# Hybrid encoder on one Trainium2 core: another order for the S5 table steps on VectorE

## The reference, cut to what matters

```python
def _s5_one_direction(ug, a_re, a_im, log_step, b_re, b_im, c_re, c_im):
    delta = jnp.exp(log_step)[:, None]
    mag = jnp.exp(a_re * delta)
    lam_re, lam_im = mag * jnp.cos(a_im * delta), mag * jnp.sin(a_im * delta)
    ...
    bb_re = coef_re[..., None] * b_re - coef_im[..., None] * b_im
    bb_im = coef_re[..., None] * b_im + coef_im[..., None] * b_re
    ...
    _, _, hr, hi = lax.associative_scan(_complex_affine_combine, (lam_re_s, lam_im_s, br, bi), axis=0)
    ...
    return jnp.einsum('bsgn,gcn->bsgc', h_re, c_re) - jnp.einsum('bsgn,gcn->bsgc', h_im, c_im)

# HGRN2: the logarithm of the forget gate, and the key
    logf = jnp.logaddexp(log_lb, log_1m_lb + jax.nn.log_sigmoid(f_pre))
    k = -jnp.expm1(logf)
```

## Time and profile before

| | before |
|---|---|
| median of 3 runs | 2617.26 us (2614.14 to 2618.61) |
| profiled execution: span from the first to the last instruction | 2610.4 us |
| the difference between the two | 6.9 us |
| TensorE busy, share of the span | 2468.0 us (95%) |
| VectorE | 1686.5 us (65%) |
| ScalarE | 1276.9 us (49%) |
| GpSimd | 218.2 us (8%) |
| mean granted TensorE clock | 0.976 of full speed; 1.00 in each 20 us stretch from 0 to 320 us |

### The profile page before, as it was taken

How to read it: one execution, slowest core, us unless ns; L and a number is a source line. 1 busy time by engine, 2 the same in 40 slices (tenths; PEclk the granted TensorE clock), 3 DMA queues, 4 the chain that set the end, 5 groups by cost and what they waited for, 6 DMA issues and landing times.

```text
span 2610.4 us, 31665 instructions
## 1 busy us (share of the span) xinstructions
PE 2468.0 (95%) x12566; PEld 1989.4 (76%) x12566; DVE 1686.5 (65%) x2051; ACT 1276.9 (49%) x1457; POOL 218.2 (8%) x236
## 2 busy tenths in 40 slices
PE   7899998999999999679799999999999999999987
PEld 4445545488888887678599888998899988998856
DVE  6897687322223334793566788668876688667865
ACT  3434434222222233752355676666765577556753
POOL 4014725000000000000100000000000000000010
PEclk9999998999999999789799999999999999999998
DMA  6556411242323223432387799778987799777961
GB/s 169 175 169 190 128 65 41 89 157 96 98 97 102 97 98 112 166 146 106 109 288 242 264 372 351 254 246 299 375 307 249 249 350 365 264 249 263 376 245 44
DMA packets 316386, 526.14 MB, mean 202 GB/s; under 512 B 19286, under 2 KB 175546, under 8 KB 313578
## 3 DMA queue, kind: packets, MB, share of 16 engines
q1 hardware_dynamic: 287162, 479.73, 53.0%
q0 software_dynamic: 5888, 25.78, 3.2%
q10 hardware_dynamic: 23184, 18.55, 2.2%
HBM read 494.46 MB, written 45.81 MB: 207 GB/s over the span
## 4 chain that ended last, share of the span: by engine, by line
PE 83%; DVE 10%; ACT 2%; issue 2%; POOL 2%; DMA 1%; POOLq 0%; ACTq 0%; DVEq 0%
PE psum L1892 28%; PE psum L1406 17%; PE psum L1952 12%; PE psum L1717 5%; PE psum L1954 5%; PE psum L1318 4%; PE psum L1293 2%; PE psum L2052 2%; PE psum L1490 1%; DVE stages L859 1%; DVE stages L869 1%; PE psum L1376 1%; DVE stages L864 1%; DVE stages L860 1%; POOL stages L1109 1%
## 5 line engine op out<-in xcount | busy, mean ns | idle before, releaser
L3500 DVE TENSOR_TENSOR stages_r<-kept,stages_r 128x2048 fp32r<-128x2048 f32 x336 | 769.3, 2291 | 239.6 <-ACT stages_r L2499 238.6
L2499 ACT ACTIVATE stages_r<-kept 128x2048 fp32r<-128x2048 f32 x336 | 637.6, 1912 | 218.7 <-PE psum L1892 104.4
L1892 PE MATMUL psum<-stages_r 128*128 128x512 f32 x3136 | 738.8, 393 | 3.2 <-issue 3.2
L1892 PEld LDWEIGHTS psum<-stages_r 128*128 128x128 f32 x3136 | 583.7, 188 | 127.0 <-issue 4.8
L1952 PE MATMUL psum<-stages_r 128*128 128x320 f32 x1792 | 465.9, 346 | 4.1 <-DVE stages L3533 3.1
L1406 PE MATMUL psum<-stages_r 128*128 128x512 f32 x1920 | 437.5, 390 | 3.2 <-ACT stages_r L2079 2.7
L1954 PE MATMUL psum<-stages_r 128*128 128x160 f32 x1792 | 423.6, 236 | 0.0
L1406 PEld LDWEIGHTS psum<-stages_r 128*128 128x128 f32 x1920 | 360.0, 188 | 79.5 <-ACT stages_r L2079 3.1
L1954 PEld LDWEIGHTS psum<-stages_r 128*128 128x128 f32 x1792 | 343.5, 192 | 2.0
L1952 PEld LDWEIGHTS psum<-stages_r 128*128 128x128 f32 x1792 | 337.7, 188 | 6.8 <-DVE stages_r L3500 3.8
L3152 DVE TENSOR_TENSOR stages_r<-kept,stages_r 128x2048 fp32r<-128x2048 f32 x54 | 123.8, 2293 | 338.7 <-ACT stages_r L2357 338.7
(11 more groups left out here) (439 smaller groups left out, 2487.0 us busy)
## 6 DMA issues: line engine op xcount, KB each, us to landing
kept<-in_moe_w_gu_dram SPq DMA_DIRECT2D x224, 1024.0 KB, 6.4
kept<-in_moe_w_down_dram SPq DMA_DIRECT2D x112, 1024.0 KB, 6.2
kept<-in_ffn_w_gu_dram SPq DMA_DIRECT2D x28, 1024.0 KB, 5.2
kept<-in_ev_w_in_dram SPq DMA_DIRECT2D x16, 1024.0 KB, 7.2
kept<-in_ffn_w_down_dram SPq DMA_DIRECT2D x14, 1024.0 KB, 5.1
s_output_maps_by_state<-stages ACTq DMA_DIRECT2D x64, 128.0 KB, 2.0
s_input_maps<-stages ACTq DMA_DIRECT2D x32, 256.0 KB, 2.5
s_output_maps<-s_output_maps_by_state SPq DMA_DIRECT2D x32, 256.0 KB, 4.7
```

The lines of the kernel that those rows point to most:

```text
L1892: m = pe.matmul(out_, a, b, start=start and n == 0, stop=stop and n == len(pairs) - 1, skip_group_check=True)
L2499: act.activation(w_high[n % WSLOTS], unit_tile(n), ACT.Copy).then_inc(s_wh, 1)
L3500: dve.tensor_tensor(w_low[n % WSLOTS], unit_tile(n), w_high[n % WSLOTS], ALU.subtract).then_inc(s_ws, 1)
```

## The change

Two edits in VectorE's program. The other engines have the same instructions in the same order as before.

1. `powers(k)` issues its four products first and its two sums last. A wait for the products still stands before each sum. Because `BQ` and `CQ` have one buffer each, and their reader is now further back, the second product of each side waits for the sum of the step before (`s_bc` at 2k - 1 and at 2k).
2. `logs_in` is split. Its first two operations stay behind the step; the third goes between the products of the input side and those of the output side of the *following* step, and the fourth between the products and the sums of that step.

```diff
-            def logs_in(d, b):
+            def logs_affine(d, b):
...
                 chain.link(dve.tensor_scalar(lf[d][:, b, :], lf[d][:, b, :], hgc[:, 6, b:b + 1], hgc[:, 5, b:b + 1],
                                              ALU.mult, ALU.add))
-                chain.settle()
-                if d:
-                    dve.wait_ge(s_lf, 1)
-                chain.link(dve.tensor_scalar(lnb4[:, b, :], lf[d][:, b, :], 1.0 / LN_SPLIT, 1.0, ALU.mult, ALU.min))
-                chain.settle()
-                dve.tensor_scalar(lf[d][:, b, :], lf[d][:, b, :], LN_SPLIT, None, ALU.max).then_inc(s_lnin, 1)
+                affine_done = chain.n
+                split_done = []
+
+                def logs_split():
+                    dve.wait_ge(chain.sem, affine_done)
+                    if d:
+                        dve.wait_ge(s_lf, 1)
+                    chain.link(dve.tensor_scalar(lnb4[:, b, :], lf[d][:, b, :], 1.0 / LN_SPLIT, 1.0, ALU.mult, ALU.min))
+                    split_done.append(chain.n)
+
+                def logs_floor():
+                    dve.wait_ge(chain.sem, split_done[0])
+                    dve.tensor_scalar(lf[d][:, b, :], lf[d][:, b, :], LN_SPLIT, None, ALU.max).then_inc(s_lnin, 1)
+
+                return logs_split, logs_floor
...
-            def powers(k):
+            def powers(k, behind=None):
...
+                if k:
+                    dve.wait_ge(s_bc, 2 * k - 1)
                 chain.link(dve.tensor_tensor(BQ.rearrange("p g d m c -> p g (d m) c"),
...
-                chain.settle()
-                dve.tensor_tensor(BP[k % 2], BP[k % 2], BQ, ALU.add).then_inc(s_bc, 1)
+                inputs_done = chain.n
+                if behind is not None:
+                    behind[0]()
                 dve.wait_ge(s_cc, k // 4 + 1)
...
+                if k:
+                    dve.wait_ge(s_bc, 2 * k)
                 chain.link(dve.tensor_tensor(CQ.rearrange("p g d m c -> p (g d) m c"),
...
-                chain.settle()
+                outputs_done = chain.n
+                if behind is not None:
+                    behind[1]()
+                dve.wait_ge(chain.sem, inputs_done)
+                dve.tensor_tensor(BP[k % 2], BP[k % 2], BQ, ALU.add).then_inc(s_bc, 1)
+                dve.wait_ge(chain.sem, outputs_done)
                 dve.tensor_tensor(CP[k % 2], CP[k % 2], CQ, ALU.add).then_inc(s_bc, 1)
...
+            logs_behind = None
             for k in range(NSTEP):
-                powers(k)
+                powers(k, logs_behind)
+                logs_behind = None
                 for d in range(2):
                     if LOGS_IN[d] <= k < LOGS_IN[d] + 4:
-                        logs_in(d, k - LOGS_IN[d])
+                        logs_behind = logs_affine(d, k - LOGS_IN[d])
```

## The result

| | before | after |
|---|---|---|
| median of the runs of this comparison | 2615.66 us (5 runs, 2614.14 to 2618.61) | 2627.21 us (5 runs, 2621.98 to 2630.10) |
| ratio after : before | | 1.004, 95% interval 1.0029 to 1.005 |
| profiled execution: span | 2610.4 us | 2625.5 us |
| steps of the stage: transposes of step 1 to those of step 31 | 150.49 us | 162.84 us |

The changed kernel is slower by 10.5 us by the ratio (7.6 to 13.1) and by 11.5 us by the medians. The prediction was 2627.1 us and a difference of 9.8 us. That the medians meet within 0.1 us is partly luck: the prediction started from 2617.26 us, and the median of before in the longer series is 1.6 us lower.

A forecast was written before the change was run, and what follows sets the result against it. TensorE and VectorE, coupled through double buffers, were taken to bound the stage by a 5.09 us loop. Step terms from +7.2 to -1.3 summed to +9.75, taken as +9.8: 2617.26 + 9.8 = 2627.1 us, range 2618 to 2636.

The forecast's parts named there:

- The loop: From VectorE's step start through input sum, transposes and kernel product to its next start: 3.81 us becomes 5.09 us.
- The settles: VectorE's waits on just-issued products: removing 80 x 0.115 = 9.2 us of its time, worth nothing in plain steps.
- The log steps: Steps 4 to 6 and 12 to 15: 5.90 us falls to 5.72, seven times -0.18 = -1.3 us.
- Steps 10 and 11, 19 and 20: First pair 11.65 us against 10.57 (+1.1), a `CP` store held back; second 11.13 against 10.73 (+0.4), behind `logs_out`.
- TensorE's idle time: Before L1364, for the input sum: 0.8 to 0.9 us with three products, 0.4 with a turned block, 23 in all.
- The stage: The 30 intervals from one step's transposes to the next: together +9.75 us, taken as +9.8 on the span.
- the wait for the stores: Input sum queued behind VectorE's wait for a `CP` store; counted in steps 10 and 11, +1.1 us.
- Pass-through: From the stage into the HGRN2 phase: delay counted in full; lower end, half of it lost in a later stage.
- A: VectorE is the bound and removing its waits pays: up to 9.2 us faster, 2608.1 us; chance 5%.
- B: At least half the delay is absorbed behind the stage, no measurable change: 2617 to 2622.5 us; chance 13%.
- C: VectorE's table operations start 0.70 and 0.755 us apart, each waiting out the last: +20 us, 2637; chance 5%.
- D: Four to eight more steps meet `CP` stores landing 1 us late: +14 to +18 us, 2631 to 2635; chance 9%.

The follow-up runs named there:

- e3: Changed kernel with the input sum one place earlier, fourth, between the two output products; ratio 0.9997 to the kernel before, stage 152.45 us.
- e5: Changed kernel with a third `BP` and a third `CP` buffer, second norm weight loaded after the stage; ratio 0.9988 to the kernel before, stage 144.84 us.
- e6: Kernel before with three buffers each for `BP` and `CP`, nothing else changed; ratio 0.9982 to the kernel before, stage 144.51 us.
- e8: Changed kernel with a third `CP` buffer only, `BP` keeping two; ratio 1.003 to the kernel before, stage 160.13 us.
- e9: Changed kernel run again unaltered, for its spread; median 2627.29 us, ratio 1.0045 to the kernel before, stage 162.49 us.
- e4: Changed kernel with a third `BP` buffer only, `CP` keeping two; ratio 1.0029 to the kernel before, stage 162.06 us.
- e2: Kernel before, input sum still third, with only the log operations spread out; median 2611.80 us, ratio 0.9988 to the kernel before, stage 146.67 us.
- e7: Kernel before with log operations spread and three buffers each for `BP` and `CP`; median 2608.92 us, ratio 0.9966, stage 140.52 us.

## Why the prediction was right, point by point

- **The loop.** Predicted: input sum 3.29 us after the step's start, a round of 5.09 us. Measured: 3.29, and 5.05 to 5.11 in every plain step but 2, 10 and 18, which wait for stores. Shown by taking it apart: one place earlier takes 0.7 us off the three-product steps (e3), a third buffer on both sides takes nearly all of them back to 4.2 (e5).
- **The settles.** Predicted to be worth nothing in plain steps. With all of them in place, three-product steps take TensorE's own 4.18 to 4.22 us in e6, which agrees. In the log steps they are worth something, and e5 shows the other side: with VectorE set free and its gaps gone, GpSimd's sum and with it ScalarE's stores came late, which the prediction had not considered.
- **The log steps.** Predicted 5.72; measured 5.73 to 5.76 in undisturbed ones. The term was -1.3 and came out at -0.27. Of the miss of 1.0 us, 0.48 is a store wait in step 5 (6.20 against 5.72). Steps 12 and 15 bring 0.19 and 0.13: step 12 had taken 5.80 and not 5.90 before, and takes 5.81 now; step 15 takes 5.84.
- **Steps 10 and 11, 19 and 20.** Predicted 11.65 and 11.13 us; measured 11.75 and 11.10 (5.65 + 6.10, and 5.09 + 6.01).
- **TensorE's idle time.** Predicted 0.8 to 0.9 us per three-product step and 23 in all; measured 0.69 and 17.2 in the 20 waits for L2878 (with 2.8 more put down to other causes). This sign was misread, not the mechanism: the idle column counts from the modelled end of the last product, 2.84 us for three, where the sum used their 2.68 from start to start. With a turned block it was 0.24 where 0.4 was named. The last sign, 246 in place of 236 us, named the last table product, but 236 was TensorE's last projection product: that one ended at 252.2 us against 235.7, and 4.1 of the 16.5 us lie ahead of step 1.
- **The stage.** +9.75 predicted, +12.35 measured. The step that failed is "the wait for the stores", which the working let decide only at step 10. It decided at steps 2 (6.02 instead of 5.09, +0.93), 5 (+0.48) and 18 (5.74, +0.65) as well: 2.06 of the 2.60 us. e8 takes these waits away and gains 2.4 against e9 and 2.7 against the change; 0.6 of the 2.7 is step 10, whose wait the working had counted.
- **Pass-through.** Counted in full, and nearly so: +12.35 of stage in one profile, 10.5 us by the ratio (7.6 to 13.1). The part from the last projection product to the end is 2374.7 us before and 2373.3 after, and 2373.8 to 2379.4 in the profiles of the experiments, so one profile does not settle a few us there. In all nine experiments the timed difference is smaller in size than that of the stage. With e4 the stage is 11.6 us longer than before and the ratio gives 7.6 us (4.7 to 10.7), with e5 it is 5.7 shorter and the ratio gives 3.1 (0.5 to 5.5); with e3 it is 2.0 longer and the ratio gives -0.8 (-3.4 to 1.6). Why is open.

The rivals:

- **A (faster)** needed a loop under 4.19 us. It was 5.09; refuted. What it supposed, a gain where VectorE is the bound, exists in the log steps and is what e2 wins: 3.8 us of stage.
- **B (no change)** needed half the delay to be absorbed; refuted by the ratio's interval.
- **C (every table operation waits out the one before)** needed starts 0.70 and 0.755 apart. They are 0.60 to 0.67; refuted. The section quoted there (the Trainium skill, VectorE: DVE Perf Modes, The DRAIN you can't avoid) is not at odds with that as a whole: it adds that "a next op that is not held starts earlier", and these operations of 0.69 us start 0.60 apart.
- **D (late stores)** happened in kind and was too large in size. Its sign, VectorE idle for stores in more than three steps, was met: there are four, of which the working had counted one (step 10). The three more are worth 2.06 us, where D had four to eight worth 4 to 8. e4 shows how near it was: with the input side freed, the same wait cost 20.4 us.

## What to carry to other kernels

When two engines hand double buffers back and forth, price an order by its loop: from a step's start to the operation that the other engine waits for, plus the way back to the next start; if that is over the other engine's own step, every step pays the difference, however idle the first engine is. So the operation that is waited for keeps its early place, and independent operations are spread over the waits, as e2 does. Then look at what stands beside the gaps: in e5, where VectorE had none left for long stretches, GpSimd's small sums took up to several us in place of 0.23, and the stores behind them came late. And widening one buffer of such a pair is not half a gain: with only `BP` tripled the stage stayed at 162 us, with only `CP` at 160, with both it fell to 145.

## What was not expected

- The second input product (L2852) took 0.74 us, and the next start came 0.67 later instead of 0.60, in 25 of 32 steps of the change (120.01 above). GpSimd's small sum, which follows ScalarE's copy of the kernel product, lies beside it. GpSimd's timeline of the changed kernel, in VectorE's step 2 and in that step:

```profile
85.79 0.23 POOL L1080 TENSOR_TENSOR stages<-stages 16x32 f32<-16x32 f32 x1 [11.94 <-ACT stages L2173]
...
119.97 0.23 POOL L1080 TENSOR_TENSOR stages<-stages 16x32 f32<-16x32 f32 x1 [4.86 <-ACT stages L2173]
```

  In the step at 84.60 us the copy and the sum came later (85.79), and L2852 at 85.21 took 0.68. In the step at 129.58 no sum ran near it, and it took 0.69. If the sum is the cause, it costs VectorE 0.06 us in each step that it falls into. These are coincidences of rows; a kernel with that sum elsewhere was not run.
- The dip of the granted clock between 70 and 80 us, in every profile but that of before, goes with a start of the stage that is 1.6 to 4.1 us later. It stands in profiles with the old order (e2, e6, e7) and with the new one, so it does not hang on the change. A comparison of two spans alone would have charged it to the kernel.
